# Head of a two-block transformer kernel: finer completion signals, a different order of small transfers, and tiles at multiples of 128 bytes

## The reference

```python
sh1, sc1, g1, sh2, sc2, g2 = split(silu(c) @ w_mod + b_mod, 6)     # the same for c_ctx
hx, hc = x * (1 + sc1) + sh1, ctx * (1 + csc1) + csh1
q, k, v = hx @ w_q, concat(hc, hx) @ w_k, concat(hc, hx) @ w_v     # 1024 x 1024 each
q, k_latent = rope(q), rope(k_latent)
```

## Time and profile before

| | |
|---|---|
| time, median of 3 runs | 1114.23 us (1114.17 to 1116.12) |
| profiled execution | 1114.73 us, span 1113.0 us |
| PE busy | 1099.3 us (99%) |
| DVE, ACT, POOL busy | 70%, 53%, 6% |
| moved by DMA | 238.31 MB, mean 214 GB/s |

### The profile page before, as it was taken

The page is one execution under the profiler, slowest core; times in us unless marked ns, Lnnn a source line. Parts: engine busy times, 40 slices in busy tenths (PEclk is TensorE's granted clock), DMA queues, the critical chain, the costliest instruction groups (busy, mean ns, idle before and its releaser), DMA issues.

```text
span 1113.0 us, 14486 instructions
## 1 busy us (share of the span) xinstructions
PE 1099.3 (99%) x5851; PEld 910.0 (82%) x5851; DVE 776.3 (70%) x1007; ACT 587.0 (53%) x821; POOL 61.4 (6%) x118
## 2 busy tenths in 40 slices
PE   8999999999999999999999999999999999999998
PEld 4688766899998887888887878878888888888886
DVE  2596588889889797877745865455566677774454
ACT  3742376563454347555534767556754466563342
POOL 0011200002121001000000000000000000000000
PEclk9999999999999999999999999999999999999999
DMA  9987740679999946667567788786524455555541
GB/s 363 403 309 249 243 163 1 208 255 349 379 383 332 350 146 232 224 211 269 183 199 126 223 177 190 155 180 134 177 76 152 152 196 203 207 189 189 189 161 38
DMA packets 111986, 238.31 MB, mean 214 GB/s; under 512 B 5712, under 2 KB 51920, under 8 KB 110640
## 3 DMA queue, kind: packets, MB, share of 16 engines
q1 hardware_dynamic: 97280, 185.42, 53.2%
q0 software_dynamic: 14352, 51.72, 13.1%
q10 hardware_dynamic: 288, 0.26, 0.1%
HBM read 236.29 MB, written 1.07 MB: 213 GB/s over the span
## 4 chain that ended last, share of the span: by engine, by line
PE 92%; DVE 3%; DMA 3%; ACT 1%; issue 0%; SPq 0%; ACTq 0%
PE ps L2068 19%; PE ps L2069 19%; PE ps L2070 19%; PE ps L2136 10%; PE ps L2138 5%; PE ps L2105 4%; PE ps L2104 4%; PE ps L2103 4%; PE ps L2253 2%; DMA raw<-in_attn_w_qkv 2%; PE ps L2388 1%; PE ps L2356 1%; DMA raw<-in_qkv_first 1%; DVE wL L1213 1%; PE ps L2277 0%; PE ps L2621 0%
## 5 line engine op out<-in xcount | busy, mean ns | idle before, releaser
L1213 DVE TENSOR_TENSOR wL<-raw,wH 128x1024 fp32r<-128x1024 f32 x326 | 394.7, 1222 | 211.3 <-ACT wH L638 208.9
L638 ACT ACTIVATE wH<-raw 128x1024 fp32r<-128x1024 f32 x326 | 340.3, 1058 | 300.4 <-PE ps L2070 196.1
L2068 PE MATMUL ps<-wH,aHL 128*128 128x512 f32 x576 | 229.3, 398 | 2.4 <-DVE aHL L1616 0.9
L2069 PE MATMUL ps<-wL,aHL 128*128 128x512 f32 (+1 forms) x592 | 229.0, 387 | 0.0
L2070 PE MATMUL ps<-wH,aHL 128*128 128x512 f32 x576 | 224.8, 390 | 0.0
L2136 PE MATMUL ps<-aHL,wH 128*128 128x512 f32 x480 | 168.8, 397 | 0.0
L2068 PEld LDWEIGHTS ps<-wH,aHL 128*128 128x128 f32 x576 | 108.1, 188 | 35.1 <-issue 7.1
L2138 PE MATMUL ps<-aHL,wL 128*128 128x256 f32 x480 | 134.1, 279 | 0.0
L2069 PEld LDWEIGHTS ps<-wL,aHL 128*128 128x128 f32 x592 | 111.3, 188 | 20.8
L2070 PEld LDWEIGHTS ps<-wH,aHL 128*128 128x128 f32 x576 | 108.1, 188 | 23.4
L2136 PEld LDWEIGHTS ps<-aHL,wH 128*128 128x128 f32 x480 | 90.1, 188 | 21.7
(11 more groups left out here) (330 smaller groups left out, 1491.7 us busy)
## 6 DMA issues: line engine op xcount, KB each, us to landing
raw<-in_ffn_w_in SPq DMA_DIRECT2D x88, 512.0 KB
modraw<-in_mod_rows POOLq DMA_DIRECT2D x80, 512.0 KB, 6.6
raw<-in_w_in SPq DMA_DIRECT2D x32, 1024.0 KB
raw<-in_ffn_w_out SPq DMA_DIRECT2D x22, 1024.0 KB
raw<-in_w_up SPq DMA_DIRECT2D x16, 1024.0 KB
raw<-in_w_down SPq DMA_DIRECT2D x16, 1024.0 KB
mod<-in_mod_first SPq DMA_DIRECT2D x8, 1024.0 KB, 16.8
raw<-in_attn_w_qkv SPq DMA_DIRECT2D x8, 1024.0 KB
```

Source lines behind the costliest of these rows:

```text
L638: nc.scalar.activation(wHigh(n), raw[:, (n // 2) % RAW, (n % 2) * 1024:(n % 2) * 1024 + 1024], ACT.Copy).then_inc(w_hi, 1)
L1213: V.tensor_tensor(wL[:, n % WL, :], raw[:, (n // 2) % RAW, (n % 2) * 1024:(n % 2) * 1024 + 1024], wHigh(n).bitcast(fp32), ALU.subtract).th ...
L2068: T.matmul(outp, xh, h, start=first, stop=False, skip_group_check=part_of)
L2069: T.matmul(outp, xh, l, start=False, stop=False, skip_group_check=part_of)
```

## The change

Half matrices get a semaphore each (`mod0_in[2 * m + h]`), and so do the first query pieces (`q_first[m]`); `adv` of an even sub-tile below 8 waits for the first piece alone and of an odd one for the second. The PE waits for the constant tables behind `mod_mm(0)` in place of ahead of it. The fillers become 3, 3 and none in place of 5, 4 and 1. In the rounds 1 and 2 the next `mod_mm` goes ahead of all of `q_mm(1, s)` and its select ahead of the last three parts. For round 3, ACT and DVE run `adv(6)` ahead of `mod_copy(3)` and `mod_put(3)`. The broadcast of c is issued after block 2 and its silu made on ACT between `adv(16)` and `adv(17)`; the second tables and the tokens are issued after block 3. The tiles `cols` and `vcol` grow, so that every large tile behind them begins at a multiple of 128 bytes.

```diff
-        cols = sb(ctx, "cols", [P, 113])
+        cols = sb(ctx, "cols", [P, P])
...
-        vcol = sb(sA, "vcol", [P, len(VECS) * KT])
+        vcol = sb(sA, "vcol", [P, 96])
...
-        mod0_in = [sem(f"mod0_in{i}") for i in range(NMOD0)]
+        mod0_in = [sem(f"mod0_in{i}") for i in range(2 * NMOD0)]
+        q_first = [sem(f"q_first{i}") for i in range(4)]
...
-                    sp.dma_start(mod0[:, 2 * m + h, :], a["mod_first"][:, m, h, :]).then_inc(mod0_in[m], 16)
+                    sp.dma_start(mod0[:, 2 * m + h, :], a["mod_first"][:, m, h, :]).then_inc(mod0_in[2 * m + h], 16)
                 sp.dma_start(xT[:, 2 * m:2 * m + 2, :], a["x_cols"][:, 2 * m:2 * m + 2, :]).then_inc(x_in[m], 16)
-                for c in range(2):
-                    sp.dma_start(raw[:, m, c * D:(c + 1) * D], a["qkv_first"][:, m, c, :]).then_inc(w_raw[m], 16)
-                if m == 1:
-                    sp.dma_start(cb[:, :], a["c"].to_broadcast([P, D])).then_inc(cb_in, 16)
+                sp.dma_start(raw[:, m, 0:D], a["qkv_first"][:, m, 0, :]).then_inc(q_first[m], 16)
+                sp.dma_start(raw[:, m, D:2 * D], a["qkv_first"][:, m, 1, :]).then_inc(w_raw[m], 32)
             sp.dma_start(ctxT, a["ctx_cols"]).then_inc(ctx_in, 16)
             for c in range(2, 6):
                 chunk(SUBS["qkv"] + 4 * c, a["attn_w_qkv"][0], c * CW)
                 if c == 2:
+                    sp.dma_start(cb[:, :], a["c"].to_broadcast([P, D])).then_inc(cb_in, 16)
+                elif c == 3:
                     sp.dma_start(cst[:, C_DIST:C_END], cst_d[:, C_DIST:C_END]).then_inc(cst2_in, 16)
                     sp.dma_start(x[:, :, :], a["x"].rearrange("b (t p) d -> p (b t) d", p=P)).then_inc(tokens_in, 16)
...
-                if n % 2 == 0:
+                if n < 8 and n % 2 == 0:
+                    act.wait_ge(q_first[n // 2], 16)
+                elif n < 8 or n % 2 == 0:
                     act.wait_ge(w_raw[(n // 2) % RAW], 32 * (n // WL + 1))
...
             for c in range(NMOD0):
+                if c == 3:
+                    adv(2 * c)
                 if c:
                     act.wait_ge(mod_sel, c)
                 mod_copy(c)
-                adv(2 * c)
+                if c < 3:
+                    adv(2 * c)
                 act.wait_ge(mod_out, c + 1)
                 hi_x(c, *mc(c))
                 adv(2 * c + 1)
-                if c == 2:
-                    act.wait_ge(cb_in, 16)
-                    nc.scalar.activation(cb[:, :], cb[:, :], ACT.Silu).then_inc(cb_ready, 1)
...
                     adv(n + 4 * c + WS + j)
+                    if (c, j) == (2, 0):
+                        act.wait_ge(cb_in, 16)
+                        nc.scalar.activation(cb[:, :], cb[:, :], ACT.Silu).then_inc(cb_ready, 1)
...
-                pe.wait_ge(mod0_in[c], 32)
                 for h in range(2):
+                    pe.wait_ge(mod0_in[2 * c + h], 16)
...
             pe.wait_ge(zeros, 1)
-            zero_mm(5, 4)
-            pe.wait_ge(cst_in, 16)
+            zero_mm(3, 4)
             pe.wait_ge(cT_ready, 2)
...
             mod_mm(0)
+            pe.wait_ge(cst_in, 16)
             mod_select(0)
-            zero_mm(4, 5)
+            zero_mm(3, 5)
...
             for s in (1, 2):
                 q_mm(0, s)
+                mod_mm(s + 1)
                 q_mm(1, s, range(1))
-                mod_mm(s + 1)
-                q_mm(1, s, range(1, 2))
                 mod_select(s + 1)
-                q_mm(1, s, range(2, 4))
-                if s == 1:
-                    zero_mm(1, 5)
+                q_mm(1, s, range(1, 4))
```

More of the change, by code:

```diff
@@ L690, in mod_copy @@
                 nc.scalar.activation(modrow[:, :], ps[:, 6, :], ACT.Copy).then_inc(mod_row, 1)
-            act.dma_start(cols[:, :], a["cols"]).then_inc(cols_in, 16)
+            act.dma_start(cols[:, 0:113], a["cols"]).then_inc(cols_in, 16)
             act.dma_start(cst[:, 0:C_DIST], cst_d[:, 0:C_DIST]).then_inc(cst_in, 16)
```

## The result

| | |
|---|---|
| time after, median of 4 runs | 1108.22 us (1106.91 to 1109.57) |
| time before beside it, median of 4 runs | 1114.9 us (1114.17 to 1116.12) |
| ratio | 0.9939, 95% interval 0.9921 to 0.9957 |
| profiled execution | 1106.91 us, span 1105.2 us (before 1114.73 and 1113.0) |

The kernel became 6.7 us faster; forecast were 4.6 us. The gain lies where the forecast put it, in the pace of the matmuls, and the head gave nothing. But the reason that I gave for the pace, multiples of 128 bytes, fell in the experiments, and so did my reading of what the head's pauses cost.

What follows compares the result with a forecast made beforehand. The PE bounds the kernel, busy 1099.3 of 1113.0 us, with transfers second in the head. Addresses -5.6 us and head +1.0 us sum to -4.6 us: 1109.6 us, range 1106.4 to 1115.8.

Steps and rivals of the forecast that it cites:

- Part 1: Head, modulation and query rounds: earlier query start and fewer fillers and waits bring block 2 2.3 us sooner, bounds 0.8 to 2.7.
- The first query product at 15.2: Start of the head: ACT waits for one query piece, 0.52 MB less, so the product starts 1.25 us sooner.
- The cost of `adv(6)` ahead: Round 3 of the head: `adv(6)` before `mod_copy(3)` delays select and queries by 0.4 us, bounds 0 and 1.9.
- block 2 begins when the rounds end: Head, after round 3: the rounds' whole saving was passed to block 2, starting 2.3 us before 49.66.
- Part 2: End of head: piece 16 still lands at 65.4 us, the silu follows it, so the head ends 1.0 us later.
- The size of the end: At `heads(1)`: the head ends 1.0 us later, bounds 0.3 us sooner to 1.0 us later.
- the pause costs the clock: Rival, before `heads(1)`: a 4 us PE pause brings the lower clock, addresses do nothing; head costs 2.8 us, 1117.0; chance 0.08.
- Transfers did not gain from the addresses: Head transfers: rows show no penalty for misaligned tiles; if 13 MB went 4% faster, 1.3 us would come back.
- Part 3: Matmul pace in the whole kernel: aligned stationary tiles save 0.015 us on each of 376 products, 5.6 us, bounds 2.6 to 7.5.
- a misaligned stationary tile: Dense matmul stages: a stationary tile off a multiple of 128 bytes may cost 0.007 to 0.020 us per product.
- Sum: Whole kernel: -5.6 us from addresses and +1.0 us from the head give -4.6 us, median 1114.23 to 1109.6.

Runs made afterwards that it cites:

- second median: The changed kernel measured once more, nothing edited, beside a version with three further head edits: 1109.31 us, ratio 0.9946.
- `adv(6)` behind: Changed kernel with `adv(6)` back behind `mod_copy(3)` and `mod_put(3)`, nothing else: 1110.34 us, ratio 0.9962.
- the silu ahead: Changed kernel with the silu of `cb` one place sooner on ACT, ahead of `adv(16)`: 1107.91 us, ratio 0.9934.
- the tokens behind block 4: Changed kernel with the silu of `cb` before `adv(16)`, and tables and tokens issued after block 4 in place of 3: 1105.89 us, ratio 0.9922.
- new head alone: Changed kernel with the three tile-size edits taken back, leaving the head's new order and signals: 1117.47 us, ratio 1.0022.
- tiles at 64: Changed kernel with `cols` grown to 144, so all moved tiles begin 64 bytes past a multiple of 128: 1115.7 us, ratio 1.0008.
- `aHL` at 32: Changed kernel with pads around `aHL`, putting it 32 bytes past a multiple of 128; tiles behind it moved by 128 bytes: 1119.66 us, ratio 1.0039.
- addresses alone: Kernel before with only the three tile-size edits of `cols` and `vcol`, its head as before: 1107.1 us, ratio 0.9928.
- `wH` at 32: Changed kernel with pads around `wH`, putting it 32 bytes past a multiple of 128; tiles behind it moved by 128: 1115.34 us, ratio 1.0001.

## Why the prediction was right, and where not

**Part 1.** The first query product at 15.2: right in the first profile (15.31); in the second the low clock near 12 us made it 15.71. The forecast had no term for that fall, nor for the wait before it: the second half of the first modulation product waits for its half matrix until about 9.0 us. Of the twelve profiles with the new head, seven show the fall, after 1.33 to 1.60 us of this wait, and five don't, after 0.69 to 1.20.

The cost of `adv(6)` ahead, 0.4 us: the wait in front of the select of round 3 was 0 to 0.77 us in the five profiles whose clock stayed up there, within the bounds. In the other four with `adv(6)` ahead it was 1.00 to 1.22 us, and the low clock followed, in the first profile with about eight matmuls 0.2 us longer, 1.6 us. That step, which charged a wait on the PE with its length alone, failed.

Block 2 came 0.2 to 1.3 us sooner in place of 2.3. Here a second step failed, that block 2 begins when the rounds end: without `adv(6)` in the way the rounds ended 2.2 to 3.0 us sooner, but block 2, which had to wait for `cL`, came only 1.7 to 2.0 sooner.

**Part 2.** Right in its mechanism, shown by the runs on the head: with `adv(6)` behind, the rounds won 1.5 us and the end nothing; with the silu ahead, the transposes came sooner; with the tokens behind block 4, piece 16 landed at least 4.5 us sooner (3.2 expected), and then the rounds' gain counted too. With their place as in the changed kernel it landed at 64.6 to 65.6 us (65.4 forecast), the silu cost 0.95. The size of the end was off: +1.0 us forecast. Aligned `cH` takes 32 x 0.0175 = 0.6 us out before the attention, so the transposes at 146.10 (before 146.43) mean a head later by 0.2 us, and those at 148.23 by 2.4. The difference is where the clock fell: near 41 us in the first profile, near 12 and 70 us in the second. The rival "the pause costs the clock", at 0.08, was thus true of the pause before `heads(1)` in one of two profiles, in the run with the new head alone and with `adv(6)` behind; it did not decide the sign, because the addresses gave more. The length of the pause alone does not decide it either, as the 3.04 us of the run with tiles at 64 show. The Trainium skill's page "TensorE: Matmul & The Clock Gate", Part 1, has activity release the clock; the falls behind pauses of 2.86, 3.07 and 3.19 us agree; why 3.04 us cost nothing, no run here shows.

Transfers did not gain from the addresses: 415, 410 and 399 GB/s in the windows 16:26, 26:41 and 50:65 us after, 418, 412 and 395 before.

**Part 3.** The term was right in place and sign and too small: 0.0195 us for a product of `hH`, `uH` in place of 0.015. 176 x 0.0194 + 128 x 0.0197 + 32 x 0.0175 + 32 x 0.007 + 8 x 0.020 = 6.9 us against 5.6. Its reason was wrong: "a misaligned stationary tile" was read from `aHL` at 0, `uH` at 96 and `cH` at 32 past a multiple of 128, and these rows can't tell a tile's own address from its distance to the moving one. The rounding to 128 worked because the rounded sizes happened to set every moved stationary tile of these products at a multiple of 256 bytes from `wH`; 128 bytes more would have given next to nothing, as the run with `aHL` at 32 shows for `hH` and `uH` (0.697 to 0.700).

By the Trainium skill's page "SBUF — State Buffer", section "Specifications (TRN2)", no address tried here would change the time, since all begin on a line of 16 bytes; the runs differ, and the measurement decides.

**Sum.** The addresses alone gave 1107.1, 7.8 us below the kernel before beside it. That is more than the 6.9 counted; 1.5 us can be in1's pace, which this run's profile and the first profile of the changed kernel had at 100.22 us for the stage and the kernel before at 101.72. By the medians the head costs the changed kernel 1.1 us, or 2.2 by its second median, where the forecast had 1.0. These differences lie within the intervals; the 2.6 us of the new head alone do not. So the head was a loss, as forecast, and a larger one; with the still larger gain of the addresses the time came 1.4 us below 1109.6.

## What to carry to other kernels

Read the pace from start to start on a saturated engine, stage by stage. When a layout changes a pace, vary the distance between the operands and the absolute place separately, and look at the stages that you did not mean to touch: two runs here gave the expected total for a wrong reason. Gains ahead of a transfer that lands at a fixed time are worth nothing until the transfer comes sooner, and the pause that they leave can cost the clock as well. Where the clock falls can change from one execution of a kernel to the next, so one profile of each kernel is too few to price such a pause.

## What of the hardware was not expected

A product of three matmuls of 512 columns takes 0.680 us when the stationary tile lies a multiple of 256 bytes from the moving one, and 0.697 to 0.700 at the remainders 32, 64, 128, 160 and 224; with 96 from `wH` and 128 from `wL` it took 0.693 to 0.700. Moving all tiles together by 32 bytes did not matter. Which of the two reads is held up was not measured. Column products, where the weights are stationary, don't follow this: in0 ran at 0.3600 us a triple of 256 columns at distance 0 and at 0.3500 and 0.3534 with `aHL` or `wH` at 32, and the pairs of in1 kept 0.3467 in both; not explained.

The granted clock fell behind short waits too: after 1.00 to 1.22 us near 39 us, not after 0 to 0.77 there; and near 68 us after 2.86, 3.07 and 3.19, but not after 3.04, nor after 0.78 to 2.36. What the PE did before differs (small modulation products with gaps in the first case, dense products in the other); no run separated length from load, and the length alone does not tell the cases apart.
